# A gated-MLP mixer's u columns by 7 block products per weight unit in place of 8, their output tiles summed in memory by DMA

## The reference

```python
def chunk_gmlp_mixer(x, w_in, b_in, ln_g, ln_b, w_s, b_s, w_out):
    z = gelu(x @ w_in + b_in)            # 576 x 6144
    u, v = jnp.split(z, 2, axis=-1)      # 3072 columns each
    v = layer_norm(v, ln_g, ln_b)        # over the 3072 columns
    sg = chunk_spatial_gate(v, w_s, b_s) # per chunk of 128 positions, lower triangular
    return (u * sg) @ w_out, v           # w_out is 3072 x 1024
...
    x = layer_norm(ALPHA * x + mix, ln1_g, ln1_b)
    x = layer_norm(ALPHA * x + hier_moe(x, ...), ln2_g, ln2_b)
    x = x + sigmoid(x @ w_gate + b_gate) * (p @ w_proj)
```

## Time and profile before

| | us |
|---|---|
| median of 3 runs | 1258.33 |
| span of the profiled execution | 1256.8 |
| TensorE busy | 1222.5 (97%) |
| VectorE busy | 833.6 (66%) |
| ScalarE busy | 559.5 (45%) |
| GpSimd busy | 165.6 (13%) |

### The profile page before, as it was taken

How to read it: one execution, slowest core, us unless ns; L and a number is a source line. 1 busy time by engine, 2 the same in 40 slices (tenths; PEclk the granted TensorE clock), 3 DMA queues, 4 the chain that set the end, 5 groups by cost and what they waited for, 6 DMA issues and landing times.

```text
span 1256.8 us, 19731 instructions
## 1 busy us (share of the span) xinstructions
PE 1222.5 (97%) x7707; PEld 1110.0 (88%) x7707; DVE 833.6 (66%) x1116; ACT 559.5 (45%) x635; POOL 165.6 (13%) x193
## 2 busy tenths in 40 slices
PE   7999999999999999999999999999999999999998
PEld 6888899999999998888878699999998888877698
DVE  4644477464554745889889786445534888888793
ACT  4422332212131312478888663211221478888651
POOL 2200010010000002022332101000002022232100
PEclk9999999999999999999999999999999999999999
DMA  9444345242432422369999563232412459999612
GB/s 336 144 162 165 116 129 180 81 140 94 134 121 79 154 74 92 143 258 363 371 385 357 204 185 106 68 101 68 135 50 90 160 214 366 386 394 345 235 51 76
DMA packets 85617, 229.76 MB, mean 183 GB/s; under 512 B 9799, under 2 KB 42703, under 8 KB 73137
## 3 DMA queue, kind: packets, MB, share of 16 engines
q1 hardware_dynamic: 66880, 179.84, 40.0%
q0 software_dynamic: 18672, 49.04, 11.0%
HBM read 210.15 MB, written 35.46 MB: 195 GB/s over the span
## 4 chain that ended last, share of the span: by engine, by line
PE 71%; DMA 13%; DVE 9%; ACT 3%; issue 2%; POOL 1%; DVEq 0%; SPq 0%; ACTq 0%; POOLq 0%
PE ps L1784 15%; PE ps L1786 15%; PE ps L1785 15%; DMA w_raw<-in_moe_w_gate_up 10%; PE ps L1835 3%; PE ps L1837 3%; PE ps L1836 3%; DVE w_lo L1182 3%; ACT w_hi L860 2%; PE ps L1895 2%; PE ps L2141 2%; PE ps L2143 1%; PE ps L2142 1%; DMA ln_params<-in_ln_b 1%; PE ps L1831 1%
## 5 line engine op out<-in xcount | busy, mean ns | idle before, releaser
L1182 DVE TENSOR_TENSOR w_lo<-w_raw,w_hi 128x2048 fp32r<-128x2048 f32 (+1 forms) x133 | 290.3, 2190 | 56.5 <-ACT w_hi L860 56.0
L1784 PE MATMUL ps<-x_hi,w_hi 128*128 128x288 f32 (+2 forms) x1024 | 304.7, 298 | 1.6 <-DVE x_lo L1658 1.6
L1786 PE MATMUL ps<-x_hi,w_lo 128*128 128x288 f32 (+2 forms) x1024 | 302.3, 295 | 0.0
L1785 PE MATMUL ps<-x_lo,w_hi 128*128 128x288 f32 (+2 forms) x1024 | 302.2, 295 | 0.0
L860 ACT ACTIVATE w_hi<-w_raw 128x2048 fp32r<-128x2048 f32 (+1 forms) x133 | 242.8, 1834 | 80.8 <-PE ps L1786 61.1
L1784 PEld LDWEIGHTS ps<-x_hi,w_hi 128*128 128x128 f32 x1024 | 193.2, 189 | 3.0 <-issue 2.4
L1785 PEld LDWEIGHTS ps<-x_lo,w_hi 128*128 128x128 f32 x1024 | 193.2, 189 | 0.1
L1786 PEld LDWEIGHTS ps<-x_hi,w_lo 128*128 128x128 f32 x1024 | 193.1, 189 | 0.0
L1784 PE MATMUL ps<-g_hi,w_hi 128*128 128x288 f32 x384 | 114.0, 297 | 1.3 <-DVE xT L1286 1.3
L1786 PE MATMUL ps<-g_hi,w_lo 128*128 128x288 f32 x384 | 113.3, 295 | 0.0
L1785 PE MATMUL ps<-g_lo,w_hi 128*128 128x288 f32 x384 | 113.1, 294 | 0.0
(11 more groups left out here) (310 smaller groups left out, 2119.3 us busy)
## 6 DMA issues: line engine op xcount, KB each, us to landing
w_raw<-in_moe_w_gate_up SPq DMA_DIRECT2D x34, 1024.0 KB, 10.7
w_raw<-in_moe_w_down SPq DMA_DIRECT2D x32, 1024.0 KB, 13.8
w_raw_more<-in_moe_w_gate_up SPq DMA_DIRECT2D x30, 1024.0 KB, 14.7
w_raw<-in_a_w_in SPq DMA_DIRECT2D x23, 1024.0 KB, 5.3
w_raw<-in_a_w_out SPq DMA_DIRECT2D x12, 1024.0 KB, 5.0
w_raw<-in_b_w_in SPq DMA_DIRECT2D x12, 1024.0 KB, 5.1
w_raw<-in_ple_w_gate SPq DMA_DIRECT2D x8, 1024.0 KB, 12.0
v_scratch<-v_stage POOLq DMA_DIRECT2D x6, 1024.0 KB, 4.5
```

Of the source, the lines that this page charges most:

```text
L1182: dve.tensor_tensor(unit_of(wlo, d), raw_unit(d), unit_of(whi, d).bitcast(f32), ALU.subtract).then_inc(split_done, 1)
L1784: pe.matmul(out, sh, mh, start=first, stop=False)
L1785: pe.matmul(out, sh, ml, start=False, stop=False)
L1786: ins = pe.matmul(out, sl, mh, start=False, stop=final)
```

## The change

Each unit of `w_in` (256 columns of u, contraction 1024) times x (288 + 288 positions) is a product of 2 x 2 blocks: the columns in two halves m, the contraction in two halves kh, the positions in two halves. The change makes it by seven block products in place of eight (Strassen's scheme in Winograd's form), 12 matmuls each. What it brings with it:

- **Weights.** Four sums of blocks of the raw unit (`sums`, four VectorE instructions of 512 columns, each waiting for the one before). A unit of `w_in` so is split twice: first the three blocks that are used as they are (`first_hi`, `first_lo`, 512 and 1024 columns), then, after the sums, the whole unit (`sum_hi`, `lo`). A round has 6 entries in place of 4, and the raw slots of this stage are three.
- **x.** Four sums of blocks of x are made in `xT` during the fifth pair of v columns (`combine_x`) and split into `x_combined_hi` and `x_combined_lo`. The latter lies over `xT`.
- **u.** The seven products are put together in `g_full` by one ScalarE copy (`first_product`) and seven VectorE instructions of 288 columns (`combined`), then four gelus of 288 columns (`u_gelu`). The products of a unit use four banks in turn, and each waits until the bank has been read.
- **The running sum.** As `xT` is taken, ALPHA times x goes to `sum_scratch` in memory during the v columns (`x_scaled`, `x_scaled_store`), ScalarE copies each output tile to a stage (`sum_copy`), and a DMA of POOL's queue adds it to `sum_scratch` in memory (`add_sum`, 5 rounds of 8 DMAs of 288 KB). Before the last rows the sum is read back into `xT` (`sum_reload`, on SP's queue). The last round makes the products of row tiles 0 and 1 together first and adds the transposes behind them.
- **Smaller moves.** The v bias is loaded in pieces; `v_cols` lies over raw slot 3; the spatial bias is added in PSUM; the router's loads and its split (`router_loads`, `router_weights`) stand behind the last round; the rounds are unrolled; output tiles 0 and 1 of a round are made by parts, as g comes.

```diff
-            def a_round(r, it, step, last=False):
-                def u_tile(fl):
-                    ...
-                    dense_tile(fl % 2, fl // 2, P * (fl % 2), KT, w8, xhi, xlo, xview).then_inc(mt_done, 1)
+            def strassen(rnd, jj, n):
+                u = 2 * rnd + jj
+                m, kh, summed, x, xh = ((0, 0, False, (xhi, xlo), (0, 0)),
+                                        (0, 1, False, (xhi, xlo), (1, 0)),
+                                        (0, 0, True, (xdh, xdl), (1, 1)),
+                                        (1, 0, True, (xdh, xdl), (0, 1)),
+                                        (1, 1, True, (xdh, xdl), (0, 0)),
+                                        (0, 1, True, (xhi, xlo), (1, 1)),
+                                        (1, 1, False, (xdh, xdl), (1, 0)))[n]
+                ...
+                if n >= 4:
+                    pe.wait_ge(c_done, CS * u + n - 3)
+                elif jj:
+                    pe.wait_ge(c_done, CS * (u - 1) + (4, 6, 7, 8)[n])
+                ...
+                products(ps[:, product_bank(rnd, jj, n), 0:HALF], terms).then_inc(q_done, 1)
+
+            def a_round(rnd):
+                for jj in range(2):
+                    for n in range(QS):
+                        strassen(rnd, jj, n)
+                        if jj and n == 3:
+                            spatial(rnd, 2)
+                        if rnd and not jj and n in (3, 4):
+                            spatial(rnd, n - 3)
+                    if rnd == 0 and jj == 0:
+                        spatial(rnd, 0)
+                        spatial(rnd, 1)
+                spatial(rnd, 3)
```

ScalarE's output tiles (`sum_tiles` on TensorE waits for `o_done` as `out_tiles` did), VectorE's sums and its first round, and the tail:

```diff
+                for mo in range(KT):
+                    sum_copy(rnd, mo)
+                    if mo == 0:
+                        first_hi(a_entry(rnd + 1, 0))
+                    if mo == 1:
+                        sum_hi(a_entry(rnd + 1, 1))
+                    if mo == 4:
+                        first_hi(a_entry(rnd + 1, 2))
...
+            def sums(d):
+                dve.wait_ge(split_done, d + 1)
+                a11, a12, a21, a22 = [quarter(raw_unit(d), m, h) for m in range(2) for h in range(2)]
+                ch.link(dve.tensor_tensor(a22, a22, a21, ALU.add))
+                ch.link(dve.tensor_tensor(a21, a21, a11, ALU.add))
+                ch.link(dve.tensor_tensor(a11, a11, a22, ALU.add))
+                dve.tensor_tensor(a12, a12, a11, ALU.add).then_inc(sums_ok, 1)
...
+            pool.wait_ge(vstate_st, AR * 32)
+            pool.wait_ge(q_done, QS * US)
             router_loads(0)
...
+                    for k0, k1 in ((0, 2), (2, 3), (3, 4)):
+                        pe.wait_ge(gl_done, gl_n - ROUND + k1)
+                        for i in range(2):
+                            ...
+                            for h in range(2):
+                                row_products(i, h, range(k0, k1), k0 == 0)
+                    pe.wait_ge(xb_ld, 32)
+                    for i in range(2):
+                        row_turns(i, 1).then_inc(mt_done, 1)
```

658 lines of the change are left out of this document (440 added, 218 removed).

## The result

The changed kernel takes 1288.62 us (median of 4 runs, 1286.68 to 1292.15) against 1258.71 us for the kernel before: 1.0234 times as long, 95% interval 1.0212 to 1.0255. It is slower, as forecast, but by 29.9 us where the forecast said 16.3, and 1288.6 lies above the range's end of 1287.

A forecast was written before the change was run, and what follows sets the result against it. TensorE's issue rate was taken to bound the rounds. Terms -19.3 + 9.3 + 12.5 + 6.8 + 3.9 + 3.1 = +16.3 us on the profiled 1256.8 gave 1273.1, forecast as a median of 1275, range 1262 to 1287.

The forecast's parts named there:

- 144 matmuls fewer: u products on TensorE: 24 fewer matmuls in a round at 0.134 us each, -19.3 us.
- first round: Before the first spatial products: TensorE idles for ScalarE's first copy and VectorE's queue up to the normalised v, +9.3 us.
- output stage: Before tile 4 in five rounds: TensorE waits 2.5 us for ScalarE's third copy, +12.5 us.
- second unit: Second unit of four rounds: VectorE's stretch of 20.0 us outlasts TensorE's 18.3, 1.7 us each, +6.8 us.
- end of the last round, up to the x_tok transposes: After the last u product: router issues and reload contention delay the first normalised rows to 19.4 us against 15.5, +3.9.
- the clock, 3.1 taken: TensorE falls to half clock after the 7.6 us gap (2.1) and partly hidden after the 4.6 us one (1.0).
- the contention in the tail, 1.0 taken: End of last round: row parameters share DMA engines with the read-back, 1.0 us taken from a range of 0 to 6.
- After that the rest moves as a block: Behind the end of the last round: experts' loads hang on splits that move with it, no further cost.
- Dense rounds: Rival: TensorE stays dense in rounds 1 to 5, both stalls gone, 1255 us; chance 0.10.
- late adding DMAs: Rival: adding DMAs take 20 us, the fifth copy of each round waits 8 us, +40, 1315 us; chance 0.06.
- dearer small instructions: Rival: small PSUM instructions cost up to 0.60 us for 288 columns, +9, 1284 us; chance 0.14.
- The clock that holds: Rival: TensorE's clock does not fall after the gaps, 1272 us; chance 0.12.

The follow-up runs named there:

- experiment 11: Changed kernel with matmuls that nobody reads in TensorE's longest waits (first spatial product, tile 4, reload, transposes of p and x_tok): 1282.50 us, 1.0197.
- Experiment 7: Changed kernel with ScalarE's high half of the summed weights behind the third copy of the output stage instead of ahead of it: 1274.79 us, 1.0121.
- experiment 9: Changed kernel with two swaps in VectorE's second-unit order (last sum ahead of gate product, spatial bias ahead of g's low half): 1291.32 us, 1.0255.
- experiments 12 and 13: Changed kernel with three load edits, later summed-weights split and VectorE swaps: 1266.43 us; the same with filler before first spatial product and x_tok transposes: 1264.05 us.
- Experiment 8: Changed kernel with 14 matmuls that nobody reads while TensorE waits before tile 4 in rounds 0 to 4: 1283.94 us, 1.0210.
- Experiments 1 to 6: Changed kernel with expert loads held back 1289.38 us; router loads later 1287.85; sum by partition 1294.52; last two together 1288.01; all three 1287.55; no reload (wrong result) 1772.
- experiment 13: Changed kernel with three load edits, later summed-weights split, VectorE swaps, and filler before first spatial product and x_tok transposes: 1264.05 us, 1.0046.
- Experiment 15: Kernel before with the changed kernel's 2.36 MB scratch tensor allocated but not used, so later scratch tensors move: 1260.01 us, 1.0014.
- experiment 10: Changed kernel with the first round's V norms of the last two row tiles on GpSimd instead of VectorE: 1286.09 us, 1.0220.

## Why the prediction was right in sign and wrong in size

By its own steps, in us of the profiled run:

| Step | predicted | measured |
|---|---|---|
| 144 matmuls fewer | -19.3 | -19.3 (spacing 0.13, as before) |
| v columns | 0 | 0 (first product at 170.48; 170.41 before) |
| first round | +9.3 | 8.16 + 1.50 - 0.44 = +9.2 |
| output stage | +12.5 | +10.9 |
| second unit | +6.8 | 3.8 + 2.9 = +6.7 |
| clock up to the last u product | +2.1 | 325.4 - 318.4 = +7.0 (experiment 11) |
| the rest of the six rounds | 0 | +2.8 (what is left; no experiment splits it) |
| end of the last round, up to the x_tok transposes | +3.9 | 25.8 - 15.5 = +10.3 |
| clock behind these, up to the first expert product | +1.0 | 1.6 + 1.2 = +2.8 |
| behind it | 0 | 716.3 - 713.4 = +2.9 |
| sum (rows rounded) | +16.3 | +33.2 |

**What was right.** The mechanism: 19.3 us of TensorE saved, and 26.8 of waits put in, at the places named, each released by the engine named, every one within 1.6 us. The waits come from the order of instructions, not from shares: VectorE is at 39.81 of 57 us and still holds TensorE up. Experiment 7 is the proof for the output stage, since one line moved takes 10.9 us of them away; experiment 9 shows it for half of the second unit's waits.

**What failed first: the clock, 3.1 taken, 9.8 in the profiled run.** The step read "The gap of 7.6 us should bring this once (2.1), the one of 4.6 partly hidden (1.0)". The first is near: experiments 12 and 13, which differ only in filler, take 305.3 and 303.6 us from the first to the last u product, 1.8 apart. What the step left out is that the waits of 2.2 us, which it had itself counted five of, could do it too. Experiment 8 prices that at 5.4. In the tail the idle time did cover the half clock up to the x_tok transposes (8.6 us from GpSimd's product at either clock); what it did not cover are the transposes and products behind them, 2.8 us where 1.0 was taken.
The Trainium skill (TensorE: Matmul & The Clock Gate, HAM oscillation — how this bites in real kernels) describes a loop whose waits throw the clock back in each pass. I had cited the page for the default state and not weighed this section against my own five waits; at the measured 1.5 a round (58.41 and 58.55 against 56.97) it would have been a rival of up to 7.5 us, 1282.

**What failed second: the contention in the tail, 1.0 taken, 7.0 in the profiled run.** GpSimd's product began at 17.2 where the step had 7.3 + 2.9 + 1.0 = 11.2. The step's own range was 0 to 6; experiments 8 and 11, with the same loads, lie inside it (product at 14.5, so 4.3), the profiled run outside. Why the same loads land up to 3.7 us apart stays open. The step thought of the reload as bytes in front of the ln loads. Experiments 1 to 6 speak for another working: 2.9 us of router issues, then two queues that take turns by packets, with reload and expert weights on one and ln and p on the other. Any one edit moves the wait to whichever load then stands against longer packets; only the three together bring the x_tok transposes to 20.4. With them and the clock held (experiment 13) the tail is +5.0, and there the router's 2.9 us are gone too: GpSimd's product still begins at 11.9 against 7.3. So 4.6 us of contention stayed even then, where the forecast had 1.0.

**What failed third: "After that the rest moves as a block".** It does not quite. In the kernels with the change and a right result the rest takes 715.8 to 719.6 us against 713.4. Experiment 15 allows some 1.5 of it for the place of the scratch tensors in memory. The remainder, 1.4 in the profiled run and more in some others, stays open: the first stretch of expert products, with the DMA engines at about 0.9 in both kernels, holds part of it (169.1 us against 167.2 up to the x_tok transposes behind it), and no wait in the trace names a cause.

**The rivals.** Dense rounds, late adding DMAs and dearer small instructions are all refuted (waits of 17.6 us, landing in 5.2 us, a record of 0.45). The clock that holds was put at 0.12 and one-sided; its mirror, a clock that falls more often, was not among the rivals at all. In the medians it is 6.1 where 3.1 was taken; 3.0 less and the time would be 1285.6, inside the range, but so small a difference is within the intervals. The upper end of 1287 had room for 3 us more of contention and dearer instructions, none for the clock.

**Two slips in the working.** In the first round 179.6 + 12.5 is 192.1, not 191.8; the trace has the spatial product at 191.92. And the estimate of 1.3 us more a round from a cost of 0.43 does not follow: 0.43 in place of 0.37 for the 8 combinations is 0.5. In the trace they start 0.37 apart.

## What to carry to other kernels

When a change puts short waits into an engine that was dense, price each of them twice: once as idle time, and once as a possible fall to half clock behind it, here 1.5 us after a wait of 2.2. How often it fell differed from profile to profile of nearly the same code (two to four rounds of five), so a saving of 3 us of idle may not show in the time until the longest waits are gone too. For the same reason, line two profiles up at several places before giving a difference at the end to one cause: here 2.8 us of a shorter tail were a load and not the clock.
When a load is on the path, look not only at the bytes ahead of it but at the packet length on the other queue: with equal counts the shorter rows lose, here 0.17 MB to 0.42. Fewer matmuls are only worth their price if the engines that feed the sums have an order, not just a share, that lets them; 19.3 us saved on TensorE bought 26.8 us of waits.

## What the runs showed of the hardware

- The same wait of 2.17 us left TensorE at full rate in two rounds and at half in three; 14 matmuls in it kept the rate in all ten rounds of two profiles (experiments 8 and 11).
- Two DMA queues with work moved 134 and 132 packets in 2 us with rows of 1,280 bytes and 4 KB, and 60 and 59 with rows of up to 9 KB against 4 KB.
- GpSimd and VectorE beside each other (experiment 10): VectorE's split of 2048 columns 3.35 us for 2.28, and 3.30 for a GpSimd multiplication of 512 columns, the one before it 1.35.
- The same 512 KB load on one queue landed 12.9 us after its issue in one profile and 10.2 in another, with the same loads around it (changed kernel and experiment 11).
- A memory tensor of 2.36 MB that nobody uses made the kernel before 0.14% slower (interval 0.05 to 0.23%).
